# Turning the rotated key and the latents before the decay and rate products, and where r k and the scores live

## The reference, cut to what matters

```python
    proj = h @ w_in[l]
    shifted = token_shift(proj[..., :RWKV_SHIFT_DIM], rwkv_mu[l])
    h_r, h_k, h_v, h_w, h_a, h_g = _split(shifted, IN_SPLITS[:6])
    c_q, c_kv, k_pe = _split(proj[..., RWKV_SHIFT_DIM:], IN_SPLITS[6:])
    # rwkv7_mixer
    w_log = -jax.nn.softplus(-(w0 + jnp.tanh(h_w) @ w2)) - 0.5     # the decay product
    a = jax.nn.sigmoid(a0 + h_a @ a2)                              # the rate product
    g = jax.nn.sigmoid(h_g) @ g2
    kk = (k * k_k); kk = kk * lax.rsqrt(jnp.maximum(jnp.sum(kk * kk, axis=-1, keepdims=True), 1e-24))
    k = k * (1.0 + (a - 1.0) * k_a)                                # the modified k
    y = rwkv7_scan(r, decay, k, v, -kk, kk * a)
    bonus = jnp.sum(r * k * r_k, axis=-1, keepdims=True) * v       # r k
    # mla_mixer
    q = (rms_norm(c_q, q_norm_g) @ w_uq)      # latents c_q, c_kv, normed
    kv = (rms_norm(c_kv, kv_norm_g) @ w_ukv)
    k_pe = apply_rope(k_pe, positions)        # the rotated key
    # then causal softmax attention, 8 heads
```

## Time and profile before

| what | us |
|---|---|
| median of three runs | 1958.35 (1955.75 to 1960.53) |
| profiled execution, whole time | 1955.12 |
| its span on the core | 1953.4 |
| TensorE busy in the span | 1874.5 (96%) |
| granted TensorE clock, mean of the span | 0.988 |

### The profile page before, as it was taken

How to read it: one execution, slowest core, us unless ns; L and a number is a source line. 1 busy time by engine, 2 the same in 40 slices (tenths; PEclk the granted TensorE clock), 3 DMA queues, 4 the chain that set the end, 5 groups by cost and what they waited for, 6 DMA issues and landing times.

```text
span 1953.4 us, 32168 instructions
## 1 busy us (share of the span) xinstructions
PE 1874.5 (96%) x12887; PEld 1564.9 (80%) x12887; DVE 1070.4 (55%) x1147; ACT 808.4 (41%) x1088; POOL 1360.4 (70%) x683
## 2 busy tenths in 40 slices
PE   5889999999999999989899999999999999999997
PEld 2668878888668898878699778888888888788886
DVE  1015547560344546876544465778888888923223
ACT  3234444444454554334322454433333434333333
POOL 2548878888248879961634598899999998844442
PEclk8999999999999999999999999999999999999999
DMA  9974545555775565533100255555555565555553
GB/s 361 380 283 166 189 157 179 188 193 192 264 272 177 167 196 187 194 118 122 44 4 4 88 172 194 175 192 184 181 193 180 185 193 178 167 194 194 193 193 129
DMA packets 174432, 352.58 MB, mean 180 GB/s; under 512 B 6735, under 2 KB 19421, under 8 KB 171773
## 3 DMA queue, kind: packets, MB, share of 16 engines
q1 hardware_dynamic: 173084, 346.84, 53.5%
q10 hardware_dynamic: 1249, 4.31, 0.6%
HBM read 349.02 MB, written 2.10 MB: 180 GB/s over the span
## 4 chain that ended last, share of the span: by engine, by line
PE 60%; POOL 17%; issue 15%; DVE 6%; ACT 1%; POOLq 0%; DVEq 0%; ACTq 0%
PE bank L929 19%; POOL WL L569 17%; PE bank L931 10%; PE bank L883 7%; PE bank L884 7%; PE bank L885 7%; PE bank L1336 6%; PE bank L1256 1%; PE bank L1266 1%; DVE CV L2429 1%; DVE CV L2434 1%; PE bank L995 1%; PE bank L1299 1%; DVE AL L2410 0%; DVE arena L2177 0%
## 5 line engine op out<-in xcount | busy, mean ns | idle before, releaser
L569 POOL TENSOR_TENSOR WL<-WR,WH 128x1024 fp32r<-128x1024 f32 (+2 forms) x516 | 1263.0, 2469 | 417.7 <-ACT WH L1556 416.4
L1556 ACT ACTIVATE WH<-WR 128x1024 fp32r<-128x1024 f32 (+2 forms) x560 | 576.4, 1036 | 780.0 <-PE bank L885 442.4
L929 PE MATMUL bank<-HX,WH 128*128 128x512 f32 x1840 | 648.6, 398 | 1.0 <-POOL WL L569 0.9
L931 PE MATMUL bank<-HX,WL 128*128 128x256 f32 x1840 | 516.9, 281 | 0.0
L929 PEld LDWEIGHTS bank<-HX,WH 128*128 128x128 f32 x1840 | 345.6, 188 | 85.1 <-POOL WL L569 2.0
L931 PEld LDWEIGHTS bank<-HX,WL 128*128 128x128 f32 x1840 | 348.1, 189 | 0.1
L883 PE MATMUL bank<-WH,HX 128*128 128x512 f32 (+2 forms) x864 | 339.8, 393 | 7.5 <-POOL WL L569 6.3
L885 PE MATMUL bank<-WH,HX 128*128 128x512 f32 (+2 forms) x864 | 331.7, 384 | 0.0
L884 PE MATMUL bank<-WL,HX 128*128 128x512 f32 (+2 forms) x864 | 331.2, 383 | 0.0
L883 PEld LDWEIGHTS bank<-WH,HX 128*128 128x128 f32 x864 | 162.7, 188 | 45.9 <-issue 12.0
L885 PEld LDWEIGHTS bank<-WH,HX 128*128 128x128 f32 x864 | 162.7, 188 | 31.0
(11 more groups left out here) (311 smaller groups left out, 2052.0 us busy)
## 6 DMA issues: line engine op xcount, KB each, us to landing
WR<-in_w_in SPq DMA_DIRECT2D x96, 1024.0 KB, 5.0
WR<-in_ffn_w_gate SPq DMA_DIRECT2D x44, 1024.0 KB, 5.2
WR<-in_ffn_w_up SPq DMA_DIRECT2D x44, 1024.0 KB, 5.1
WR<-in_ffn_w_down SPq DMA_DIRECT2D x44, 1024.0 KB, 5.1
arena<-in_w_ada SPq DMA_DIRECT2D x64, 512.0 KB, 10.5
WR<-in_w_out SPq DMA_DIRECT2D x32, 1024.0 KB, 5.1
WR<-in_w_ada SPq DMA_DIRECT2D x16, 1024.0 KB, 5.0
WR<-in_w_in SPq DMA_DIRECT2D x12, 768.0 KB, 4.4
```

The costliest lines, as they stand in the source:

```text
L569: eng.tensor_tensor(half(WL, n % NSLOT, *w), half(WR, n % NSLOT, *w), half(WH, nth(n) % 2, *w), ALU.subtract).then_inc(ready, 1)
L929: pe.matmul(bank[:, :].rearrange("p (h n) -> p h n", h=2), wh[:, k, o], hx[:, :, kk, :], start=kk == 0, stop=False, skip_group_check=True)
L931: last = pe.matmul(bank[:, 0:L], wl[:, k, o], hx[:, 0, kk, :], start=False, stop=kk == KT - 1, skip_group_check=True)
L1556: act.activation(half(WH, nth(n) % 2, *w), half(WR, n % NSLOT, *w), ACT.Copy).then_inc(hi_ready, 1)
```

## The change

Five edits that belong together:

- TensorE turns the rotated key and the latents directly behind r, k and v, ahead of the decay and rate products, into banks 2 and 3 instead of 4 and 5. It needs banks 2 and 3 read out (`raw_taken` 23), not all of them. Of the decay and rate products, groups 2 and 3 wait for all turned tiles to be taken (`xT_taken` 58). MLA's part 0 then waits for 4 of `rw_small_took` (its second half for 8), and the head sums for all 16.
- ScalarE does the same in its order: the two sigmoids of the gate, `take_feature` from banks 2 and 3, then the 16 sigmoids of `low_rank_out`.
- GpSimd makes r k straight behind the modified k; the wait for piece n_g2 is gone there (the masks keep theirs).
- RK moves to the arena at 7168 to 9216; S2 and Pr2 move to the weight slot of piece n_wo2 + 1; PT2 moves to the arena at 24224, where the rotation's scratch was.
- SP's load of that slot waits for the last of attention's transposed probabilities (`probsT_ready` 24) instead of `bonus_ready` 4.

```diff
-        S2, Pr2, PT2 = at(7168, 2, SPAN), at(7936, 2, SPAN), at(8704, 2, SPAN)
+        RK = at(7168, 8, L)
+        PT2 = at(24224, 2, SPAN)
-        RK = WR[:, (n_wo2 + 1) % NSLOT, :].rearrange("p (f n) -> p f n", f=8)
+        S2, Pr2 = (WR[:, (n_wo2 + 1) % NSLOT, 768 * i:768 * (i + 1)].rearrange("p (h n) -> p h n", h=2) for i in range(2))
...
-                    sp.wait_ge(bonus_ready, 4)
+                    sp.wait_ge(probsT_ready, 3 * HEADS)
...
-            pool.wait_ge(piece_done, n_g2)
             own.mark(pool.tensor_tensor(RK, R_, K_, ALU.mult))
...
+            pe.wait_ge(raw_taken, RAW_C - 4)
+            pe.wait_ge(kpx_ready, 4)
+            all_to_feature(KPX.rearrange("p t a n -> p t (a n)"), 2, 2, 24)
+            pe.wait_ge(c_normed, 2 * TT)
+            for q in range(2):
+                all_to_feature(CQ[:, 2 * q:2 * q + 2, :], 4, 2, 25 + 2 * q)
             pe.wait_ge(rw_mid, 1)
             pe.wait_ge(raw_taken, RAW_C)
...
             for g in range(4):
+                if g == 2:
+                    pe.wait_ge(xT_taken, 2 * 29)
...
-            pe.wait_ge(rw_small_took, 16)
-
-            pe.wait_ge(kpx_ready, 4)
-            all_to_feature(KPX.rearrange("p t a n -> p t (a n)"), 2, 4, 24)
-            pe.wait_ge(c_normed, 2 * TT)
-            for q in range(2):
-                all_to_feature(CQ[:, 2 * q:2 * q + 2, :], 4, 4, 25 + 2 * q)
-            pe.wait_ge(xT_taken, 2 * 29)
+            pe.wait_ge(rw_small_took, 4)
...
                     pe.wait_ge(rw_masks, 1)
+                    pe.wait_ge(rw_small_took, 16)
...
+                if part == 0:
+                    pe.wait_ge(rw_small_took, 8)
...
+            act.activation(HG0, HG0, ACT.Sigmoid).then_inc(rw_mid, 1)
+            act.activation(HG1[0:32, :], HG1[0:32, :], ACT.Sigmoid).then_inc(rw_mid, 1)
+            take_feature([KPT[:, k, :] for k in range(2)], 24, first=2)
+            for q, name in enumerate(("mla_q_norm_g_2", "mla_kv_norm_g_2")):
+                take_feature([CT[:, 4 * q + k, :] for k in range(4)], 25 + 2 * q, [col(name, k) for k in range(4)], first=2)
             for r in range(8):
                 low_rank_out(r)
-            act.activation(HG0, HG0, ACT.Sigmoid).then_inc(rw_mid, 1)
...
```

More of the change, by code:

```diff
@@ L1587, in _, with take_feature @@
                                ACT.Copy).then_inc(xT_taken, 2)
-            def take_feature(dsts, base, gains=None):
+            def take_feature(dsts, base, gains=None, first=4):
                 for g in range(len(dsts) // 2):
@@ L1593, in take_feature @@
                         k = 2 * g + f
-                        act.activation(dsts[k], BANK[4 + (base + g) % 2][:, f * L:(f + 1) * L], ACT.Copy,
+                        act.activation(dsts[k], BANK[first + (base + g) % 2][:, f * L:(f + 1) * L], ACT.Copy,
                                        scale=gains[k] if gains else 1.0).then_inc(xT_taken, 1)
```

## The result

The changed kernel takes 1946.73 us (median of five runs, 1943.10 to 1947.83); the kernel before, run beside it, 1958.35 (five runs, 1955.49 to 1966.35). The ratio is 0.9937, with a 95% interval of 0.9923 to 0.9951: 11.6 us shorter. The sign was forecast, but the time lies 0.2 under the range's low end: 7.4 were forecast, 11.6 came.

What follows compares the result with a forecast made beforehand. The prediction took TensorE's chain to bound the kernel, with 16.14 us between v's last product and part 0. Gain 8.9 less 1.5 for VectorE gives 7.4: 1958.35 - 7.4 = 1951.0 us, range 1946.9 to 1957.0.

Steps and rivals of the forecast that it cites:

- TensorE's stage: Last product of v to MLA's part 0: part 0 starts at 865.6 instead of 874.47, a gain of 8.9 us.
- The other bound, 7.4: Same stretch of TensorE: gain only 7.4 us if the 20 transposes keep the 5.02 us of the lower clock.
- the 876.2 of the prediction: Time at which MLA's part 1 needs its query weights; their later loads were to stay hidden, some 4 us to spare.
- VectorE's collision: Rotation of the queries meets GpSimd's r k: held 3.1, multiplies 0.8, 3.9 us late, 1.5 off the gain.
- The free 2.4: Idle time of ScalarE and VectorE before attention: up to about 2.4 us of the gain costs them nothing.
- From attention on I move everything by the same amount: Attention to the kernel's end: every stage keeps its length, so no gain or loss was counted there.
- the median of the runs lies 3.2 above that execution: Step from the profiled execution, 1955.12 us, to the median of the runs, 1958.35, before subtracting 7.4.
- rival 2: Rotation of the queries: no collision with GpSimd's large product, gain 8.9 us, 1949.5; chance 0.14.
- 1 and 4 (the clock falls): Lower clock between 858 and 865: gain 5.5, 1952.9, chance 0.14; over MLA's parts too: 4.6 or 12.9 slower, chance 0.04.
- The rule weighed there: Transposes don't count as busy like matmuls, so the new order would look idle until 861.9 and lose its clock.
- 3 (held by all of r k): Rotation of the queries: VectorE waits for all of r k, gain 0.1 us, 1958.3, no change; chance 0.10.
- 5 (transposes wait): Transposes wait for VectorE until 860.85: 2.5 us off TensorE's gain, leaving 6.4, about 1952.5; chance 0.04.

Runs made afterwards that it cites:

- te_only: The kernel before with only TensorE's and ScalarE's new order; r k, its slot and the waits as before: 1946.91 us, ratio 0.9948.
- rk_only: The kernel before with only r k's new place, the scores in the weight slot and SP's new wait: 1958.73 us, ratio 1.0013.
- raw_all: The changed kernel, with the transposes waiting until VectorE has read all banks of r, k and v: 1947.26 us in one execution.
- rk_late: The changed kernel, with GpSimd waiting for the rotated queries before r k: 1945.99 us, ratio 0.9946.
- before_2: The kernel before, unchanged, profiled a second time: 1958.61 us.
- after_2: The changed kernel, unchanged, profiled once more: 1944.92 us.

## Why the prediction was right, and where it was wrong

**TensorE's stage: right.** 8.9 forecast, 9.0 to 9.1 measured. Part 0 came 7.01 behind the last product of v; 7.27 was the sum. The sum had the last copy done at +4.7 us and TensorE free of transposes at +3.6; the rows give 866.21 (+4.3) and 865.34 (+3.4). The other bound, 7.4, was not met: the transposes ran at the full clock. Part 1 began 10.58 behind part 0 and didn't wait for its weights; the 876.2 of the prediction fits that, but 7.17 + 3.73, which count an overlap twice, would give 876.5.

**VectorE's collision: the mechanism right, the size wrong.** The rotation met r k, VectorE's first product was held until GpSimd's large one ended, and the multiplies behind it cost little. Forecast: held 3.1, 0.8 for the multiplies, 3.9 late, 2.4 free, 1.5 lost. Measured: the rotation took 7.33 (890.88 to 898.21) instead of 4.49 (te_only, 891.24 to 895.73), so 2.84 late: some 2.3 of it in the first four products, 0.5 in the rest. The free 2.4 was right; of the difference, some 0.3 to 0.4, 0.32 shows. **This is the first step that failed**: "VectorE is then 3.9 us late ... 1.5 come off". The multiplies were taken at their bound ("at most 0.15 more each"), and r k's large product was to end 25.0 behind part 0, where it ended 24.24 behind it: it began 0.6 earlier than worked out and took 4.52, under the 4.7 that was called its least. Because a fixed 2.4 is subtracted, an excess of 1.1 in the lateness made the loss five times too large. The Trainium skill, page "SBUF — State Buffer", section "Who interferes with whom", says that where the two engines meet on their shared port, the one that issues first holds it for its whole instruction; the held 2.28 us agree with that, the multiplies' 0.5 is what measurement adds.

**Attention: no term, and 1.7 us.** "From attention on I move everything by the same amount" is **the second step that failed**. The trace of before already held the stretch at 0.50 in the gate products, but the prediction used the clock only where the change lies. What can be said is how much (40.6 against 38.95), what it is (3.4 us at half the clock, 1.7 lost) and where it came: in five of five executions with TensorE's old order (rk_only among them), in none of five of the changed kernel, none in te_only and raw_all, and one in rk_late. It isn't r k beside attention (te_only, rk_only). The timed runs speak for the 1.7 too: without it the stages would give 9.1, under the 9.6 to 11.9 that both intervals share. Why the new order mostly avoids the stretch stays open, and so does whether it is the order that does it. In all six executions that have it, it begins at one place of the program, 26.1 to 26.7 us behind the first scores. TensorE waited ahead of that place in both orders, in all thirteen profiled executions for VectorE and for 0.95 to 0.96 us. A window of before_2, just ahead of its stretch:

```profile
955.00:957.00 2.00, 1.04 (x8) 0.62 (x6) 1.97 (x4) 0.00 (x0) 1.79 (x4) 1.00 0.80 240
```

The same place in after_2, which had no such stretch:

```profile
944.00:948.00 4.00, 2.91 (x15) 1.91 (x15) 3.93 (x9) 0.73 (x4) 0.00 (x0) 1.00 0.00 0
```

Both show TensorE idle for about a microsecond while VectorE is busy, so the wait alone doesn't decide it.

**From profile to median.** The step "the median of the runs lies 3.2 above that execution" is a plain difference; the prediction didn't know that 2.4 of it can be the rhythm of the wide products, and no run shows that it is. Subtracting from the one profiled execution and comparing profile with profile gives 8.4, which looks like a forecast met; it is 10.5 from the three stages around the change, less 2.4 for the rhythm, plus 1.5 behind the recurrence, less 1.2 ahead of the wide products: a match by luck.

**The range.** With the collision at 0.3 the forecast would have been 1949.8, with attention 1948.1. The low end was rival 2 less the spread of the runs of before, and no case in it ran shorter from attention on; the text named such a change as what would make it wrong and gave it no price.

**The rivals.** 1 and 4 (the clock falls): refuted by the window 858.00 to 923.80, and the granted clock was 1.00 from 858 to 876 in all five executions of the changed kernel. The rule weighed there, from the Trainium skill, page "TensorE: Matmul & The Clock Gate", section "Part 4: PE-mode transpose", that transposes don't count as busy the way matmuls do, does not describe this stage: the clock stayed at 1.00 through a stretch of only transposes (861.75 to 865.27), in the one execution of raw_all even behind 2.58 us without work. 2 (no collision) is nearest in time, 1949.5, but not in cause; the rotation was longer. 3 (held by all of r k) would have begun the rotation 33.1 behind part 0; it began 22.0 behind it and ended 29.3 behind it. 5 (transposes wait): the first one starts at 861.75, and raw_all shows what rival 5 would have looked like, at 2.8 instead of 2.5.

**r k's move brings nothing by itself.** It was costed as a loss, and rk_only (no change) and te_only (the whole gain without it) show that no part of the gain hangs on it.

## What to carry to other kernels

Where TensorE stands between a producer and its own next work, turn first what needs only banks that are already read, and put the products whose results others must process behind it; the read-out then overlaps with work that was to be done anyway. When a delay is set against a free margin, work out both ends of the difference and not only of the delay, since its relative error is the larger one. Before a time is moved "by the same amount", list every stretch at the lower clock in the trace of before, and profile the kernel twice if it can be had: one execution can sit 2 us to one side by chance.

## What the runs showed of the hardware that was not expected

The same wide products run in one of two rhythms by the execution, at a granted clock of 1.00: 145 or 146 of L929's products in 50 us, or 142 or 143, which makes 201.5 or 203.8 us of the stage. Of 13 profiled executions of six kernels five had the quick one. What selects it is open.

A stretch of 3.4 us at the lower clock (955.8 to 959.2 in before, 947.7 to 951.1 in rk_late) cost 1.7 us where TensorE had no idle time. All thirteen profiled executions have the same wait of TensorE's ahead of it, 0.95 to 0.96 us, and six have the stretch. Behind the recurrence, near 1700 us, such stretches come and go between executions of one kernel.
